# Output stage of a hybrid SSD/attention/PEER layer: weight splits and half of the squares placed elsewhere in the order of work

## What is computed

```
merged = sigmoid(g_a) * y_a + sigmoid(g_b) * y_b2
x = x + gate1 * (merged @ w_o)
h = rmsnorm(x, norm2_w) * (1 + scale2) + shift2
q = h @ w_pq                       # queries of the PEER routing
s = einsum(q, sub_keys); top 16 per head and half
```

## Time and profile before

| | us |
|---|---|
| median of 3 runs | 2667.16 |
| lowest and highest run | 2665.56 and 2667.79 |
| span of the profiled execution | 2665.9 |
| PE, DVE, ACT, POOL busy in the span | 2488.3, 2093.9, 1137.6, 811.1 |

### The profile page before, as it was taken

The page is one execution under the profiler, slowest core; times in us unless marked ns, Lnnn a source line. Parts: engine busy times, 40 slices in busy tenths (PEclk is TensorE's granted clock), DMA queues, the critical chain, the costliest instruction groups (busy, mean ns, idle before and its releaser), DMA issues.

```text
span 2665.9 us, 38926 instructions
## 1 busy us (share of the span) xinstructions
PE 2488.3 (93%) x14998; PEld 2188.1 (82%) x14998; DVE 2093.9 (79%) x3683; ACT 1137.6 (43%) x1945; POOL 811.1 (30%) x621
## 2 busy tenths in 40 slices
PE   6889999999999987997999887999999999999997
PEld 5778888888888877996886786888888888888886
DVE  3767777724777765543999796999999999999999
ACT  4335656535666654314444582333333332333333
POOL 0000000004565550100343583443334433343431
PEclk9999999999999988998999998999999999999999
DMA  7421121233233224332123489999999999999996
GB/s 305 174 104 70 68 99 70 86 135 121 84 137 100 86 85 166 140 135 103 65 70 109 151 244 382 417 416 417 416 418 412 418 404 411 405 413 417 417 408 247
DMA packets 166408, 621.48 MB, mean 233 GB/s; under 512 B 14896, under 2 KB 83280, under 8 KB 105808
## 3 DMA queue, kind: packets, MB, share of 16 engines
q1 hardware_dynamic: 124752, 340.03, 34.5%
q0 software_dynamic: 36864, 268.45, 24.5%
q10 hardware_dynamic: 4608, 10.52, 1.3%
HBM read 559.26 MB, written 59.56 MB: 232 GB/s over the span
## 4 chain that ended last, share of the span: by engine, by line
PE 73%; DVE 15%; DMA 5%; ACT 3%; issue 3%; SPq 0%; DVEq 0%; POOL 0%; PEldq 0%; PEld 0%; ACTq 0%; POOLq 0%
PE c_pp L862 8%; PE p_py L2620 5%; PE p_py L2622 5%; PE p_py L2621 5%; PE p_pa L2603 4%; PE p_pa L2605 4%; PE p_pa L2604 4%; PE o_ps L1715 4%; PE s_pg L1407 4%; PE e_ps L2420 4%; PE p_py L2634 3%; DMA w_raw<-in_w_stream 2%; PE g_ps L1070 2%; PE a_ps L810 2%; DVE p_uv L2741 2%
## 5 line engine op out<-in xcount | busy, mean ns | idle before, releaser
L2585 POOL DMA_INDIRECT p_uv<-in_uv_rows,merged x256 | 398.6, 1557 | 619.4 <-DVE merged L2758 558.8
L2603 PE MATMUL p_pa<-h2D,w_hi 128*128 128x384 f32 x896 | 318.8, 356 | 20.6 <-DVE w_lo L2712 20.5
L2758 DVE SCALAR_TENSOR_TENSOR merged<-p_uv,p_sw,merged 128x1024 f32<-128x1024 f32 x256 | 328.7, 1284 | 7.2
L2741 DVE CUSTOM_DVE_ANT_0 p_uv<-p_uv,merged 128x1024 f32<-128x1024 f32 x256 | 308.1, 1220 | 11.3 <-DMA p_uv<-in_uv_rows,merged 11.3
L2605 PE MATMUL p_pa<-h2D,w_lo 128*128 128x384 f32 x896 | 302.8, 338 | 0.0
L2604 PE MATMUL p_pa<-h2D,w_hi 128*128 128x384 f32 x896 | 302.7, 338 | 0.0
L2654 ACT ACTIVATE w_hi<-w_raw 128x2048 fp32r<-128x2048 f32 x110 | 210.4, 1912 | 154.7 <-PE p_py L2622 89.3
L2712 DVE TENSOR_TENSOR w_lo<-w_raw,w_hi 128x2048 fp32r<-128x2048 f32 x110 | 251.8, 2289 | 24.0 <-ACT w_hi L2654 23.7
L2620 PE MATMUL p_py<-w_hi,p_wh 128*128 128x512 f32 x672 | 265.6, 395 | 1.7 <-DVE w_lo L2712 1.7
L2622 PE MATMUL p_py<-w_hi,p_wl 128*128 128x512 f32 x672 | 265.3, 395 | 0.0
L2621 PE MATMUL p_py<-w_lo,p_wh 128*128 128x512 f32 x672 | 265.1, 394 | 0.0
(11 more groups left out here) (408 smaller groups left out, 6101.4 us busy)
## 6 DMA issues: line engine op xcount, KB each, us to landing
w_raw<-in_w_stream SPq DMA_DIRECT2D x174, 1024.0 KB
g_pairs<-e_st SPq DMA_DIRECT2D x5, 4096.0 KB, 16.2
p_g<-g_pairs SPq DMA_DIRECT2D x64, 320.0 KB
t_ada<-in_w_ada SPq DMA_DIRECT2D x16, 1024.0 KB, 7.1
xc_dram<-c_xc SPq DMA_DIRECT2D x8, 1284.0 KB
p_ve<-in_v_early SPq DMA_DIRECT2D x8, 1024.0 KB, 13.4
r_ur<-in_u_early ACTq DMA_DIRECT2D x14, 512.0 KB, 3.7
s_xx<-xc_dram SPq DMA_DIRECT2D x8, 642.0 KB, 6.3
```

What stands on the lines that cost most here:

```text
L2585: nc.gpsimd.indirect_dma_start(uv[:, k % RING, :], None, K.uv_rows, bass.IndirectOffsetOnAxis(K.sidx[:, t, c:c + 1], 0)).then_inc(K.gather ...
L2603: nc.tensor.matmul(ps_a[m][:, :], wh[:, k, cols], K.h2D[0][:, k, :], start=k == 0, stop=False)
L2741: nc.vector.tensor_tensor_reduce(uv[:, b, 0:D], uv[:, b, 0:D], K.hrow[:, t, :], 1.0, 0.0, ALU.mult, ALU.add, sa[:, at:at + 1]).then_inc(do ...
L2758: nc.vector.scalar_tensor_tensor(ys[:, t, :], uv[:, b, D:2 * D], sw[:, at:at + 1], ys[:, t, :], ALU.mult, ALU.add).then_inc(v_done, 1)
```

## The change

- The low part of U_O+2 is made by DVE right behind the first residual, not behind all five.
- The squares are done in two halves of 512 columns. ACT sums the first halves of all five tiles behind the high part of U_O+3, the second halves where the whole squares stood. The two sums are added by the instruction that scaled the single one; the division by 1024 goes into the root's own scale.
- Behind the first halves ACT takes a root of a constant into an unused cell.
- The low part of U_PQ goes from t = 0 of DVE's loop to t = 4, where that of U_PQ+1 stood; that of U_PQ+1 goes to the head of DVE's program in `phase_route`.
- `modulated` waits for the transposes ahead of each of its 8 activations, not of each 4. The programs of SP, PE and POOL are as they were.

```diff
@@ scalar
+        def first_squares(t):
+            act.wait_ge(res, t + 1)
+            if t >= 2:
+                act.wait_ge(sq0_done, t - 1)
+            nc.scalar.activation(xn[t % 2][:, 0:512], x[:, t, 0:512], ACT.Square, accum_out=ss[:, 0, t:t + 1]).then_inc(sq0_done, 1)
         def squares(t):
             ...
-            nc.scalar.activation(xn[t % 2], x[:, t, :], ACT.Square, accum_out=ss[:, t:t + 1]).then_inc(sq_done, 1)
+            nc.scalar.activation(xn[t % 2][:, 512:D], x[:, t, 512:D], ACT.Square, accum_out=ss[:, 1, t:t + 1]).then_inc(sq_done, 1)
         def root(t):
-            nc.scalar.activation(ss[:, t:t + 1], ss[:, t:t + 1], ACT.Sqrt).then_inc(rt_done, 1)
+            nc.scalar.activation(ss[:, 0, t:t + 1], ss[:, 0, t:t + 1], ACT.Sqrt, scale=1.0 / D).then_inc(rt_done, 1)
         for n in range(U_O, U_PQ - 1):
             S.hi(act, n + 2, n % 2)
+            if n == U_O + 1:
+                for t in range(NT):
+                    first_squares(t)
+                nc.scalar.activation(unused[:, :], K.ones[:, 0:1], ACT.Sqrt)
@@ vector
         def normed(t):
+            dve.wait_ge(sq0_done, t + 1)
             dve.wait_ge(sq_done, t + 1)
-            nc.vector.tensor_scalar(ss[:, t:t + 1], ss[:, t:t + 1], 1.0 / D, EPS, ALU.mult, ALU.add).then_inc(ms_done, 1)
+            nc.vector.tensor_scalar(ss[:, 0, t:t + 1], ss[:, 0, t:t + 1], ss[:, 1, t:t + 1], EPS * D, ALU.add, ALU.add).then_inc(ms_done, 1)
         ...
         for t in range(NT):
             residual(0, t)
-        S.lo(dve, U_O + 2, 0)
+            if t == 0:
+                S.lo(dve, U_O + 2, 0)
         S.lo(dve, U_O + 3, 1)
         residual(1, 0)
         for t in range(NT + 1):
             ...
-            if t == 0:
+            if t == 4:
                 S.lo(dve, U_PQ, 0)
-            if t == 4:
-                S.lo(dve, U_PQ + 1, 1)
             if t:
                 split(t - 1)
@@ phase_route, vector
+        S.lo(dve, U_PQ + 1, 1)
         stage([nc.vector.tensor_copy(name[:, 0, 0:1], K.iota[:, 61:62]),
```

More of the change, by code:

```diff
@@ L1865, in phase_mix_out @@
     hf = lambda t: hfS[t] if t < NTS else K.h32[:, :, (t - NTS) * P:(t - NTS + 1) * P]
-    ss = sb("x_ss", [P, NT])
+    ss = sb("x_ss", [P, 2, NT])
     ps = [ctx.enter_context(nc.psum_tensor(f"x_ps{t}", [P, 2 * UC], F32)) for t in range(NT)]
@@ L1871, in phase_mix_out @@
     r_done = sem("x_r"); xn_done = sem("x_xn"); tr_done = sem("x_tr"); hf_done = sem("x_hf_done"); hh = sem("x_hh"); hl = sem("x_hl")
-    x_out = sem("x_out")
+    x_out = sem("x_out"); sq0_done = sem("x_sq0")
     half = lambda t, h: 2 * t + h
+    unused = sb("x_unused", [P, 1])
     block = K.block
@@ L1890, in _, with part @@
         K.leave(sp)
+    def part(t):
+        return (K.h2S, slice(t * P, (t + 1) * P)) if t < NTS else (K.h2D, slice((t - NTS) * P, (t - NTS + 1) * P))
     @block.gpsimd
@@ L1946, in squares @@
                 act.wait_ge(tr_done, 2 * (t - 1))
-            nc.scalar.activation(xn[t % 2], x[:, t, :], ACT.Square, accum_out=ss[:, t:t + 1]).then_inc(sq_done, 1)
+            nc.scalar.activation(xn[t % 2][:, 512:D], x[:, t, 512:D], ACT.Square, accum_out=ss[:, 1, t:t + 1]).then_inc(sq_done, 1)
         def root(t):
             act.wait_ge(ms_done, t + 1)
-            nc.scalar.activation(ss[:, t:t + 1], ss[:, t:t + 1], ACT.Sqrt).then_inc(rt_done, 1)
+            nc.scalar.activation(ss[:, 0, t:t + 1], ss[:, 0, t:t + 1], ACT.Sqrt, scale=1.0 / D).then_inc(rt_done, 1)
         def modulated(t):
-            for h in range(2):
-                n = half(t, h)
+            for kd in range(KD):
+                n = half(t, kd // 4)
                 act.wait_ge(tr_done, n + 1)
[L1957 to L1961, removed]
+                nc.scalar.activation(hf(t)[:, kd, :], ps_x[n % 3][:, kd % 4, :], ACT.Identity,
+                                     scale=K.mul2[:, kd, group(t):group(t) + 1],
+                                     bias=K.add2[:, kd, group(t):group(t) + 1]).then_inc(hf_done, 1)
         for n in range(U_O, U_PQ - 1):
             S.hi(act, n + 2, n % 2)
+            if n == U_O + 1:
+                for t in range(NT):
+                    first_squares(t)
+                nc.scalar.activation(unused[:, :], K.ones[:, 0:1], ACT.Sqrt)
         for t in range(NT):
@@ L1988, in normed @@
         def normed(t):
+            dve.wait_ge(sq0_done, t + 1)
             dve.wait_ge(sq_done, t + 1)
-            nc.vector.tensor_scalar(ss[:, t:t + 1], ss[:, t:t + 1], 1.0 / D, EPS, ALU.mult, ALU.add).then_inc(ms_done, 1)
+            nc.vector.tensor_scalar(ss[:, 0, t:t + 1], ss[:, 0, t:t + 1], ss[:, 1, t:t + 1], EPS * D, ALU.add, ALU.add).then_inc(ms_done, 1)
             dve.wait_ge(rt_done, t + 1)
-            nc.vector.reciprocal(ss[:, t:t + 1], ss[:, t:t + 1]).then_inc(r_done, 1)
+            nc.vector.reciprocal(ss[:, 0, t:t + 1], ss[:, 0, t:t + 1]).then_inc(r_done, 1)
             dve.wait_ge(r_done, t + 1)
@@ L1995, in normed @@
                 dve.wait_ge(tr_done, 2 * (t - 1))
-            nc.vector.tensor_scalar(xn[t % 2], x[:, t, :], ss[:, t:t + 1], None, ALU.mult).then_inc(xn_done, 1)
+            nc.vector.tensor_scalar(xn[t % 2], x[:, t, :], ss[:, 0, t:t + 1], None, ALU.mult).then_inc(xn_done, 1)
         def split(t):
             dve.wait_ge(hf_done, KD * (t + 1))
-            part = K.h2S if t < NTS else K.h2D
-            tc = slice(t * P, (t + 1) * P) if t < NTS else slice((t - NTS) * P, (t - NTS + 1) * P)
-            nc.vector.tensor_copy(part[0][:, :, tc], hf(t)).then_inc(hh, 1)
+            (high_part, low_part), tc = part(t)
+            nc.vector.tensor_copy(high_part[:, :, tc], hf(t)).then_inc(hh, 1)
             dve.wait_ge(hh, t + 1)
-            nc.vector.tensor_tensor(part[1][:, :, tc], hf(t), part[0][:, :, tc].bitcast(F32), ALU.subtract).then_inc(hl, 1)
+            nc.vector.tensor_tensor(low_part[:, :, tc], hf(t), high_part[:, :, tc].bitcast(F32), ALU.subtract).then_inc(hl, 1)
         dve.wait_ge(x_in, 48)
```

## The result

The changed kernel is slower. Its first four runs have a median of 2681.45 us (2676.64 to 2682.93) against 2667.47 of the kernel before beside them; the ratio is 1.0045, with a 95% interval of 1.0033 to 1.0057. That is 12 us more by the ratio, where 7.2 was forecast, and above the stated range. Two later sets, of six runs each, gave 2677.38 against 2668.11 (ratio 1.0032, 1.0020 to 1.0044) and 2677.32 against 2668.94 (1.0030, 1.0018 to 1.0042), 8 us by the ratio; both of these medians lie just inside the stated range, which ends at 2677.5. The direction and the mechanism held; the size forecast was too small, and the first set lies higher than the other two.

The account below looks back on a forecast made before the run. PE, busy 93% of the span, was taken as the bound; -5.91 and -0.41 at DVE's end, routing 13.3 later than that, and +0.3 for the clock gave +7.2, so 2674.4 us, range 2669.5 to 2677.5.

Parts of the forecast that it names:

- the first write behind the load: SP's queue: load and first write together take 7.14 us to the second write's issue; bounds 4.2 less or 2.9 more.
- the two-sum instruction: DVE's adding of the two half sums in the output stage; named in a heading, with no price of its own.
- Early low part: Low part of U_O+2 early: PE's stall there goes and the clock stays up, gain 5.91 us.
- Early table: ACT's root table load of 1.28 us moves into idle time; already hidden, so gain nothing, cost nothing.
- Halved squares: Half the squares early on ACT: 0.41 us goes in the one round where DVE idles for them.
- Writes behind the low part: SP's load and five writes wait for U_PQ's late low part; SP's leave opens routing, PE starting 6.9 us later.
- The clock in routing: PE's restart at half clock as routing begins: up to 0.5 us more or less, taken as +0.3.
- The sum: DVE's end earlier by 5.91 and 0.41, routing 13.3 later than that: +6.9, with the clock +7.2.
- B: Rival: SP's writes go faster, the first not held by the load; +2.7, with the clock 2670.2 us; chance 0.10.
- A: Rival: SP is not last to leave, the output stage ends with DVE at 1239.55; 2660.9 us, chance 0.06.
- C: Rival: PE still stalls at U_O+2 and the 5.91 stays lost; +13.1, 2680.3 us, chance 0.04.
- The transfer's length: SP's 512 KB writes: 2.61 us each by measurement; the skill's 3.2 us would make the sum 2.4 larger.

Follow-up runs that it names:

- b_early_low: The kernel before with only the low part of U_O+2 moved behind the first residual; 2661.92 us against 2668.11, ratio 0.9981.
- b_query_lows: The kernel before with only the low part of U_PQ moved to t = 4 and that of U_PQ+1 into routing; 2683.72 us, ratio 1.0061.
- a_load_last: The changed kernel with SP's load of U_PQ+2 put behind the five writes; 2661.76 us, ratio 0.9981 of the kernel before.
- a_writes_first: The changed kernel with SP still waiting for U_PQ's low part ahead of the writes, but the load behind them; 2675.83 us against 2668.99 before, ratio 1.0029.
- a_low_back: The changed kernel with only the low part of U_PQ put back to t = 0; 2663.39 us against 2668.99 of the kernel before, ratio 0.9986.
- c_high_in_routing: a_low_back with ACT's high part of U_PQ+1 also moved to the head of routing; 2663.75 us against 2668.99 of the kernel before, ratio 0.9981.
- d_pe_kept_busy: c_high_in_routing with 44 unused identity matmuls on PE behind the transposes of tiles 1 to 4; 2664.05 us against 2668.94 before, ratio 0.9980.
- a_again: The changed kernel run once more, no edit; 2677.38 us against 2668.11 of the kernel before, ratio 1.0032.

## Why the prediction was right and where it was wrong

The mechanism was right, and what failed is the size of terms in the sum: the first write behind the load, the restart of the clock, and the two-sum instruction. They make the difference that the traces show; a further 3 to 4 us of the first result stay open.

- **Early low part.** Right. From first residual to first transpose it is 40.24 us in place of 46.01, 5.8 earlier for 5.9 foretold, stall and clock together; b_early_low alone carries it. The small rest is at the seam, 0.54 from start to start (with 0.26 of issue) where 0.35 was taken.
- **Early table.** Right, nothing.
- **Halved squares.** The step that failed is the two-sum instruction. The prediction names it in a heading and gives it no price; it takes 0.06 more than the scaling, three times on the ring, and the wait shrank by 0.35, not 0.41. So 0.41 became 0.17, and DVE ended 5.9 to 6.0 us earlier, not 6.3.
- **Writes behind the low part.** The mechanism, its place and the releaser were right, and b_query_lows and a_load_last show it from both sides. From DVE's low part to the opening of routing it was 1255.18 - 1236.87 = 18.3 where 17.7 had been summed. The pace of 2.61 held to 0.02. The mis-sized term is the first write behind the load: taken as 6.77, it measured 7.38, 8.02 and 7.43 in the three traces, inside the bounds given but always above the value taken. It was also the term named as least certain. Why it is longer here than in the kernel before is not shown.
- **The clock in routing.** The term of +0.3, with at most 0.5, was too small. PE stood at half clock for 3.1, 6.1 and 6.2 us of its start in the three traces of the changed kernel, 3.8 in that of before; so the first head, from PE's start to the first search, differs by -0.3, +1.0 and +1.1 us. The bound had been drawn from one other restart (4.9) as if it were the longest. Nor does the pause ahead set the length: 18.48 us of idle PE came before the 3.1, 18.53 before the 6.2.
- **The sum.** In the stage the changed kernel loses 7.9, 8.6 and 8.0 us at PE's start, where 6.9 had been foretold. DVE's end, 0.4 to 0.5 less early than foretold, and the first write, 0.6 to 1.3 longer, make that difference. At the first search it is 7.6, 9.6 and 9.1 where 7.2 had been foretold; there the clock comes in. The remaining 3 to 4 us of the first result's 12 are in none of these traces, and did not come back in twelve further runs of the same kernel.
- **The range.** Its own terms, B and the upper bound of the first write, each with the clock's 0.3 and 1 us of scatter, give 2669.2 to 2678.3 and not 2669.5 to 2677.5; the first result lies above both. The 1 us of scatter came from three runs within 2.2 us. The kernel before spreads over 8 us in 22 runs (2665.66 to 2673.63), and its later medians are 2668 to 2669. The range was too narrow by that, whatever the mechanism. Taken as differences of medians, the later sets are 9.3 and 8.4 over before, between the 2.3 and 10.3 that the range spans above 2667.2; the first set is 14.0 over.
- **The rivals.** A (DVE still last) fell: 18.3 us behind the low part, not under 4.4. B was built as a kernel (a_writes_first) and is what it said, 3.4 us of stage in place of 7.9, but the change doesn't do it. C (PE stalls still) fell at the first row, though its time, 2680.3, is the nearest to the first result.
- **The transfer's length.** The Trainium skill ("DMA: Bandwidth & Descriptors", section "Anatomy of one DMA — SWDGE (gpsimd) path") would have given 3.2 us for each write, by the prediction's estimate; the traces of this stage say 2.60 to 2.63, before and after.

Five kernels in which DVE opens routing stand at 0.9980 to 0.9986 of the kernel before (b_early_low, a_load_last, a_low_back, c_high_in_routing, d_pe_kept_busy), and their intervals overlap. The first of them needs one moved line, and nothing else in the change is shown to add to it.

## What to carry to other kernels

When a producer is moved later, list every queue that waits for it, and then everything that stands behind that wait in the same queue: here a load whose data ACT took only 39 us after its issue (1276.36) held five writes that had been ready, and the writes held a barrier. SP's idle time ahead of the barrier, 8.7 us, was the slack that the move could spend, and it moved SP's end by 16.5 (from 1237.25 - 1175.30 = 61.95 behind the first residual to 1255.12 - 1176.63 = 78.49; each end is the last write's issue and 2.61). The 7.8 beyond the slack are the loss, to 0.1 us. And a fix may be in the order of the queue rather than in the move: with the load last, the same low part in the same late place costs nothing.

## What the runs showed of the hardware

- A 512 KB write from the chip to HBM takes 2.60 to 2.63 us from issue to the next issue, wherever only its landing held the next; behind a 1 MB load in the same queue it takes 6.8 to 8.0 (6.77 before, 8.02 in a_again), and 2.61 again when the load is put behind it.
- A DVE instruction on one column that takes a second column as its scalar runs 0.21 us (the changed kernel, L2003), with two constants 0.15 (before, L1990).
- Half clock at a restart of PE lasted between 3.1 and 6.2 us in the same program, behind pauses of 18.48 us (for the 3.1) and 18.53 us (for the 6.2). Matmuls added ahead of a pause of 2.4 us (d_pe_kept_busy) brought the granted clock back to 1.00; it stayed there through the pause, and fell to 0.50 as work began behind it.
